# SSD's sums of squares added on VectorE first, and mLSTM's denominators in one matmul for both chunks

## The reference

```
for l in range(2):                       # T = 256 tokens, D = 1024, fp32
    x = x + 0.5 * swiglu(rms_norm(x), ffn1)
    u = rms_norm(x) @ w_in[l]
    y = concat(ssd_mixer(u_ssd), mlstm_mixer(u_ml), rwkv7_mixer(u_rw))
    x = x + y @ w_out[l]
    x = x + 0.5 * swiglu(rms_norm(x), ffn2)
# end of ssd_mixer, y is (256 tokens, 1024), two groups of 512 features
    y = y * silu(z)
    yf = y.reshape(b, t, 2, 512)
    yf = yf * rsqrt(mean(yf * yf, axis=-1) + 1e-6)
    return yf.reshape(b, t, 1024) * norm_g
# inside mlstm_mixer, per head and chunk of 128 tokens (2 chunks, 4 heads)
    qk = einsum(q, k) * w_intra
    num = einsum(qk, v) + einsum(q, c_prev) * w_inter
    den = sum(qk, axis=keys) + einsum(q, n_prev) * w_inter
    h = num / maximum(abs(den), exp(-m_t))
```

## Time and profile before

| | |
|---|---|
| median of 3 runs | 1820.75 us (1820.26 to 1820.97) |
| profiled execution | 1821.4 us |
| its span, first to last instruction | 1819.6 us |
| mean granted TensorE clock | 0.978 of full speed |
| TensorE busy | 1744.4 us, 96% |
| VectorE busy | 1228.8 us, 68% |
| ScalarE busy | 888.1 us, 49% |
| GpSimd busy | 355.4 us, 20% |

### The profile page before, as it was taken

The page is one execution under the profiler, slowest core; times in us unless marked ns, Lnnn a source line. Parts: engine busy times, 40 slices in busy tenths (PEclk is TensorE's granted clock), DMA queues, the critical chain, the costliest instruction groups (busy, mean ns, idle before and its releaser), DMA issues.

```text
span 1819.6 us, 37064 instructions
## 1 busy us (share of the span) xinstructions
PE 1744.4 (96%) x16066; PEld 1661.9 (91%) x16066; DVE 1228.8 (68%) x2050; ACT 888.1 (49%) x1560; POOL 355.4 (20%) x308
## 2 busy tenths in 40 slices
PE   6999999999899999999999999989999998789997
PEld 6999988887899999999998888789999987789997
DVE  5886675766567775678576675665787575569964
ACT  5664435323346554565444432345565555356652
POOL 3552000000112651256100000011355200011110
PEclk9999999999799999999999999989999999889999
DMA  8655522211147565565552311014565542235442
GB/s 297 237 217 192 210 93 93 94 36 37 48 163 269 214 222 195 201 262 207 191 204 77 109 71 48 25 62 172 209 255 203 212 165 97 90 124 184 179 153 103
DMA packets 44498, 282.96 MB, mean 156 GB/s; under 512 B 6064, under 2 KB 6704, under 8 KB 17712
## 3 DMA queue, kind: packets, MB, share of 16 engines
q1 hardware_dynamic: 44336, 280.60, 42.3%
HBM read 279.53 MB, written 1.05 MB: 154 GB/s over the span
## 4 chain that ended last, share of the span: by engine, by line
PE 83%; DVE 11%; ACT 4%; issue 1%; DMA 1%; POOL 0%; SPq 0%; DVEq 0%; ACTq 0%; POOLq 0%
PE bank L489 20%; PE bank L491 20%; PE bank L490 20%; PE bank L975 7%; PE bank L1571 3%; DVE WL L480 2%; ACT WH L475 2%; PE bank L520 1%; PE bank L1838 1%; PE bank L1115 1%; DMA ring<-wst 1%; DVE XC L1044 1%; PE bank L1848 1%; PE bank L677 0%; DVE ML L1342 0%
## 5 line engine op out<-in xcount | busy, mean ns | idle before, releaser
L489 PE MATMUL bank<-XNH,WH 128*128 128x256 f32 (+1 forms) x2176 | 621.6, 286 | 20.6 <-DVE XNL L566 12.7
L480 DVE TENSOR_TENSOR WL<-ring,WH 128x2048 fp32r<-128x2048 f32 (+1 forms) x235 | 509.9, 2171 | 188.3 <-ACT WH L475 188.0
L491 PE MATMUL bank<-XNH,WL 128*128 128x256 f32 (+1 forms) x2176 | 617.7, 284 | 0.0
L490 PE MATMUL bank<-XNL,WH 128*128 128x256 f32 (+1 forms) x2176 | 615.7, 283 | 0.0
L475 ACT ACTIVATE WH<-ring 128x2048 fp32r<-128x2048 f32 (+1 forms) x235 | 406.3, 1730 | 232.9 <-PE bank L491 182.3
L489 PEld LDWEIGHTS bank<-XNH,WH 128*128 128x128 f32 x2176 | 414.2, 190 | 26.0 <-DVE XNL L566 12.7
L490 PEld LDWEIGHTS bank<-XNL,WH 128*128 128x128 f32 x2176 | 415.5, 191 | 0.0
L491 PEld LDWEIGHTS bank<-XNH,WL 128*128 128x128 f32 x2176 | 415.5, 191 | 0.0
L489 PE MATMUL bank<-HH,WH 128*128 128x256 f32 x880 | 246.4, 280 | 0.7 <-POOL HL L872 0.6
L490 PE MATMUL bank<-HL,WH 128*128 128x256 f32 x880 | 246.2, 280 | 0.0
L491 PE MATMUL bank<-HH,WL 128*128 128x256 f32 x880 | 246.1, 280 | 0.0
(11 more groups left out here) (466 smaller groups left out, 2513.4 us busy)
## 6 DMA issues: line engine op xcount, KB each, us to landing
ring<-wst SPq DMA_DIRECT2D x206, 1024.0 KB, 4.8
ring<-wst SPq DMA_DIRECT2D x80, 704.0 KB, 4.2
LP<-lp SPq DMA_DIRECT2D x1, 1872.0 KB, 8.5
LP<-lp SPq DMA_DIRECT2D x1, 1792.0 KB, 8.8
X<-xin SPq DMA_DIRECT2D x2, 512.0 KB, 4.5
out<-X SPq DMA_DIRECT2D x4, 256.0 KB, 2.6
C<-cst SPq DMA_DIRECT2D x1, 193.0 KB, 10.6
AL<-cst SPq DMA_DIRECT2D x1, 192.0 KB, 10.7
```

What stands on the lines that cost most here:

```text
L480: e.do.tensor_tensor(WL[:, slot[q], 0:n], ring[:, i % NSLOT, 0:n], WH[:, slot[q], 0:n].bitcast(F32), ALU.subtract).then_inc(*w_dve.up("low ...
L489: e.do.matmul(o, WH[:, s, cols], xh, start=first, stop=False)
L490: e.do.matmul(o, WH[:, s, cols], xl, start=False, stop=False)
L491: return e.do.matmul(o, WL[:, s, cols], xh, start=False, stop=last)
```

## The change

In the mLSTM strand, the two matmuls of ones with a chunk's weights become one over both chunks, and the order within the step changes. In the ssd strand, VectorE adds each group's four tiles of squares down to one, in two additions (512 columns, then 256), in step 25, which was empty; TensorE then sums one tile per group and chunk, waiting for the additions' event in place of the squares'.

```diff
--- before.py
+++ after.py
@@ -1159,11 +1159,10 @@
                 yield
                 e.wait_ge(*s_act.on("state", l, h))
                 e.do.matmul(b[:, 0:128], vt[:, 0, :], wT[:, 0, :], start=True, stop=True)
-                e.do.matmul(b[:, 256:384], ones, wT[:, 0, :], start=True, stop=True)
+                e.do.matmul(b[:, 256:512], ones, ww, start=True, stop=False)
+                e.do.matmul(b[:, 384:512], nst.to_broadcast([128, 128]), qw, start=False, stop=True)
                 e.do.matmul(b[:, 128:256], vt[:, 1, :], wT[:, 1, :], start=True, stop=False)
-                e.do.matmul(b[:, 128:256], cT, qw, start=False, stop=True)
-                e.do.matmul(b[:, 384:512], ones, wT[:, 1, :], start=True, stop=False)
-                e.do.matmul(b[:, 384:512], nst.to_broadcast([128, 128]), qw, start=False, stop=True).then_inc(*s_pe.up("out", l, h))
+                e.do.matmul(b[:, 128:256], cT, qw, start=False, stop=True).then_inc(*s_pe.up("out", l, h))
                 yield
             yield
             yield
@@ -1855,11 +1854,9 @@
             yield
             yield
             for g in range(2):
-                e.wait_ge(*d_act.on("sq", l, g))
+                e.wait_ge(*d_dve.on("squares", l, g))
                 for c in range(2):
-                    for i in range(4):
-                        s = T * i + c * 128
-                        m = e.do.matmul(b[:, 2 * g + c:2 * g + c + 1], (xd, xe)[g][:, s:s + 128], ones[:, 0:1], start=i == 0, stop=i == 3)
+                    m = e.do.matmul(b[:, 2 * g + c:2 * g + c + 1], (xd, xe)[g][:, 128 * c:128 * c + 128], ones[:, 0:1], start=True, stop=True)
             m.then_inc(*d_pe.up("sums", l))
             yield
             yield
@@ -1965,6 +1962,12 @@
                 yo = Y[:, 4 * g:4 * g + 4, :]
                 e.do.tensor_tensor(yo, yo, XC[:, 4 * g:4 * g + 4, :], ALU.mult).then_inc(*d_dve.up("gated", l, g))
             yield
+            for g in range(2):
+                q = (xd, xe)[g]
+                e.wait_ge(*d_act.on("sq", l, g))
+                e.do.tensor_tensor(q[:, 0:512], q[:, 0:512], q[:, 512:1024], ALU.add).then_inc(*d_dve.up())
+                e.wait_ge(*d_dve.last())
+                e.do.tensor_tensor(q[:, 0:256], q[:, 0:256], q[:, 256:512], ALU.add).then_inc(*d_dve.up("squares", l, g))
             yield
             e.wait_ge(*d_pe.on("sums", l))
             dve_rsqrt(e, d_dve, b[:, 0:4], 4, 1.0 / 512, EPS, 128, ("rstd", l))
```

## The result

The changed kernel took **1830.10 us** (median of 4 runs, 1827.52 to 1831.10), the kernel before beside it 1820.71 (4 runs, 1820.26 to 1820.97). The ratio is 1.0047, with a 95% interval of 1.0035 to 1.006: slower by 0.35% to 0.6%. The profiled execution took 1830.15 us, its span is 1828.4. The forecast was +6.0 us, 1826.8, in a range of 1824.0 to 1830.4.

A forecast was written before the change was run, and what follows sets the result against it. It took VectorE's queue to bound the SSD readout, hiding TensorE's sums. Two layers' readouts 3.05 us late, less 0.1 us for mLSTM, gave +6.0 us: 1826.8 us for the median, range 1824.0 to 1830.4.

The forecast's parts named there:

- The bound is VectorE's queue: At the SSD readout, VectorE's queued low half and state scalings come last, hiding 5.24 us of TensorE sums.
- The adds land behind L480 and two L1708: In SSD step 25, the additions stand behind w_out's low half and two of the four state scalings on VectorE.
- 2.2 us for the adds: Four VectorE additions in the SSD strand, priced at 0.69 or 0.42 us each, put 2.2 us per layer on the path.
- Sums at half clock, readout 3.05 us late: Four SSD sums become exposed on TensorE at clock 0.50; readout starts at 485.13 instead of 482.09.
- The wait at the readout: After the change VectorE waits about 0.8 us for TensorE at the SSD readout, where it had not waited.
- Behind that, nothing makes up a delay: From the readout to w_out's second part, one chain; TensorE then has no idle time to make up a delay.
- mLSTM 0.1 us: One wide matmul for two in mLSTM saves 0.01 us a head, 0.1 over eight; upper bound 1.8 us.
- Sum +6.0: Both layers' late readouts less the mLSTM saving: 1827.4 us for the profiled execution, 1826.8 for the median.
- rival B: Behind the readout, TensorE's clock stays low longer, costing up to 2.2 us more per layer: 1831.2 us; chance 0.11.
- a sign of being wrong: TensorE's clock returning elsewhere relative to the rows behind the readout would show the forecast wrong; no size given.
- The range: Whole kernel between 1824.0 and 1830.4 us, with under 2 in 10 left outside.
- Rival A: Additions ahead of w_out's low half run in VectorE's 2.92 us wait; readout unmoved, 0.1 gained, 1820.7 us; chance 0.09.

The follow-up runs named there:

- x3_early: The whole change, but with VectorE's additions in step 24, ahead of the low half of w_out's first block; 1821.30 us, ratio 0.9996 to the kernel before.
- x9_before_low: The kernel before, with the low half of w_out's first block moved behind the reciprocal root on VectorE; 1822.73 us, ratio 1.0002.
- x4_dummy: The kernel before plus four same-sized VectorE additions on dead data in step 25 that nobody waits for, 16 sums kept; 1826.95 us, ratio 1.0025.
- x2_ssd: Only the SSD part of the change, mLSTM as in the kernel before; 1829.22 us, ratio 1.004.
- x1_mlstm: Only the mLSTM part of the change, SSD as in the kernel before; 1822.18 us, ratio 1.0004.
- the second: The changed kernel itself, measured and profiled once more without alteration; 1828.21 us, ratio 1.004 to the kernel before.
- x10_change_low: The whole change, with the low half of w_out's first block also moved behind the reciprocal root; 1816.62 us, ratio 0.9977 to the kernel before.
- x7_sixteen: The kernel before plus four VectorE additions on dead data, with TensorE's 16 sums per layer waiting for them; 1840.47 us, ratio 1.0113.

## Why the prediction was right, point by point

- *The bound is VectorE's queue; 5.24 us of sums are hidden.* Shown by x3_early (same work, earlier place, no loss) and x9_before_low (the queue taken away, the sums bind after 0.5 us of gain, the half microsecond of slack I had read).
- *The adds land behind L480 and two L1708.* They did, to the instruction.
- *2.2 us for the adds.* Measured 0.69, 0.43, 0.68 and 0.42, with the gaps as taken: 480.80 to 483.00. The trace sides with the rows of L1947 and L1686. The table in the Trainium skill's page VectorE: DVE Perf Modes, section on the TRN2 errata, would have given an estimated 0.59 and 0.33.
- *Sums at half clock, readout 3.05 us late.* The prediction's own times give 3.04 (485.13 less 482.09). Measured 2.98 and 2.99, of which 0.73 are the sums (x4_dummy against x2_ssd). The wait at the readout was forecast at 0.8 and is 0.77. TensorE ran the sums at half clock, with records of 0.352 us in place of the 0.25 at full clock, behind an idle of 8.32 us. This agrees with the Trainium skill's page TensorE: Matmul & The Clock Gate, section on HAM oscillation, by which a gap on TensorE makes the next burst start at the lower clock.
- *Behind that, nothing makes up a delay.* The mixer ends grew by 2.99 and 3.21 us; 680.9 us lie between the first stretch and the second gate in both kernels.
- *mLSTM 0.1 us.* 0.02 a head, 0.16 in all, by the profile; below what timing can tell (x1_mlstm).
- *Sum +6.0.* The change's own share is 6.2 in the first profile and 6.8 in the second (3.40 and 3.35). What was too small is the term for the clock behind the readout, which I had set at zero and given to rival B: 0.0 to 0.4 us a layer in these profiles, 0.6 and 0.8 in x4_dummy. B was half right. The clock's return did move by more than the work, which the prediction had named as a sign of being wrong: by 0.1 and 0.5 us more than the readout in the first profile, 0.9 and 0.8 in the second. At 0.45 us for each this gives the 0.0 to 0.4, and never the 2.2 us that I had allowed. The prediction had also read the return in the kernel before as 488.3; it was 488.5.
- *The range.* The first measurement, 1830.10, lies 0.3 us below its upper edge. In the one execution profiled there, the last stretch was 3.6 us longer, most of it by the clock in the second block, a place that the prediction hadn't looked at; that it still fell inside is in part luck. The second one, +7.0, lies inside with room.
- *Rival A* did not come true, since the additions stand behind L480, but the slack ahead of L480 that it named is real: x3_early is that rival built, and it takes the time of before. Fewer sums pay only where the low half doesn't stand ahead of the readout: with it moved behind the root, the change gives 4.5 us (x10_change_low), and the same move without the change gives nothing that the timing shows (x9_before_low).

What stays open: why the first four runs of the kernel before lay within 0.7 us while later sets spread over 8. The difference between executions that I could see in profiles was in the low-clock stretches; I haven't profiled enough executions to say that it is all of it. The surplus of x7_sixteen's median stays open too.

## What to carry to other kernels

A stage that takes 5 us on an engine isn't worth 5 us if the next reader comes later for another reason: look at what stands ahead of the reader in its own queue. When work is moved to a strict queue, its place there decides more than its length; 2.2 us of additions cost 3 us behind one instruction and nothing ahead of it. And when the new work shortens a hidden stage, find the move that makes that stage bind (here a low half put beside the rows), since only the two together pay.

## What I had not expected of the hardware

One program's executions spread by 8 us (1818.62 to 1826.57 over 27 runs of the kernel before), and two profiled executions of the changed kernel differ by 3.87 us in a stretch of some 586 us that the change doesn't touch, with granted clock 0.96 against 0.97. In the stretches shown the granted clock was at 0.50 in both, and came back to full at different places. So in a kernel like this one, whose TensorE pauses often, a single profiled pair can misplace some 4 us: compare stretches cut at the same instructions before believing a difference of spans.
